# Attention's weighted values accumulated in PSUM bank 5 in place of bank 0

## The chip, the cores and the metric

The kernel runs on one core of a Trainium2 chip. The metric is device time in microseconds (us) of that core, the median of several executions. The engines named below are PE (TensorE, matmuls), ACT (ScalarE), DVE (VectorE), POOL (GpSimd) and SP (SyncE, which issues the DMAs). Each runs its own list of instructions in order and they meet through semaphores. PE writes its results into PSUM, of which this kernel uses eight banks of 128 x 512 floats.

## What is computed

A hybrid encoder trunk of two layers on 512 tokens of width 1024. In each layer one input projection feeds three mixers that run side by side: sliding-window attention with sinks, retention, and a Mamba-2 scan. Their outputs are concatenated and projected back; then comes a gated MLP. The part that the change touches is the attention:

```
def swa_sink_attention(q, k, v, sinks, attn_bias):
    ...
    logits = jnp.einsum('bcqhgd,bckhd->bchgqk', qc, kb).astype(jnp.float32) * (HEAD_DIM ** -0.5)
    logits = logits + attn_bias.reshape(A_KV_HEADS, G, CHUNK, A_WIN_CHUNKS * CHUNK)[None, None]
    ...
    p = jax.nn.softmax(jnp.concatenate([logits, sink], axis=-1), axis=-1)[..., :-1]
    out = jnp.einsum('bchgqk,bckhd->bcqhgd', p.astype(v.dtype), vb)
    return out.reshape(Bn, S, A_WIDTH)
```

The last einsum, the weighted values, is the step called AV. The retention reads its values centred over the head's width; that step is called RV.

## The kernel before

Activations lie with features on the 128 partitions and the 512 tokens along the free axis. A matrix product is done in "units" of one 128-wide block of output features: for each 128-wide block of the inner dimension three matmuls of 128 x 512, high part of the weights by high and by low part of the input, low part of the weights by high part of the input. The weights come by DMA in packs of four tiles into four slots (`w_raw`); ACT makes the high part `w_hi` (line 481), POOL the low part `w_lo` (line 378). Units write the two banks `dense0` and `dense1` in turn. All the mixers' small products share six further banks, `M[0]` to `M[5]` ("mix" in the profile).

The order on every engine comes from one hand-written list, `SCHEDULE` (line 80). Each engine walks through it once per layer and does its own share of each step, so that a step that is early in the list is early on every engine. D*n* are units of the projections. The piece in question, for each layer:

```
    "SB2 SA3 D16 D17 SB3 AS0 RV0 D18 RV1 AX0 D19 RV2 AT0 AS1 D20 RV3 AX1 AV0 D21 AT1 AS2 D22 AX2 AV1 "
    "SN0 D23 SX0 AT2 AS3 D24 AX3 AV2 SN1 D25 SX1 D26 AT3 RP0 D27 AV3 RP1 D28 RP2 D29 RP3 D30 RA0 D31 "
```

The attention works on four blocks of 128 queries, n = 0 to 3:

- AS*n*: PE computes scores into banks 0 and 1 and the transposed values into bank 4; DVE reads the scores out (line 910), takes the maximum and subtracts it (lines 920 to 926); ACT copies the values (line 580) and takes the exponentials (lines 583, 584).
- AX*n*: DVE sums, inverts and scales (lines 931 to 934).
- AT*n*: PE transposes the weights into banks 2 and 3; ACT copies them to `pt` (line 588).
- AV*n*: PE multiplies values and weights, four matmuls of 64 x 256 (line 1283), half of them on bank 2's copy and half on bank 3's; ACT splits off the high part (line 593, helper on line 498), DVE the low part (line 943), whose end frees the bank.

RV*n* is a step of the retention: PE multiplies one unit's result by a centring matrix into bank 5 (line 1296), ACT copies it to `vtok` (line 596), whose end frees the bank. RP*n* (rotary, bank 4; DVE line 954), RA*n* and RB*n* (retention; RA uses bank 0, RB bank 5 among others) follow. D20 to D23 are the scan's gate: DVE evacuates each (line 796), ACT takes its Silu (line 525), DVE multiplies it in (line 804), ACT squares the product (line 529). SN*n* sums squares in bank 4.

`BANKS` (line 96) says which banks a step uses. `bank_uses` numbers the uses of each bank in the order of `SCHEDULE`, and `take` (line 1095) lets PE wait until the use before has been read: `m_free[b]` counts the releases of bank b, `m_ready[b]` the results in it. ACT and DVE wait for the same numbers, through `ready`.

Of the kernel before, what the change touches and what calls it, by code (L numbers as in the profile page):

```python
# [88 lines left out]
def step_of(name):  # L89
# [5 lines left out]

BANKS = {
# [3 lines left out]
}  # L100

# [69 lines left out]
def build(nc, a, out):  # L171
    f32, f32r = mybir.dt.float32, mybir.dt.float32r
    ALU, ACT, AX = mybir.AluOpType, mybir.ActivationFunctionType, mybir.AxisListType
    with ExitStack() as ctx:
# [235 lines left out]
        def _(act):  # L410
# [60 lines left out]
            with act.Fori(0, DEPTH) as l:  # L471
# [28 lines left out]
                for name in SCHEDULE:  # L500
# [37 lines left out]
                    elif step == "TK":  # L538

                        act.wait_ge(dt_in, l + 1)  # L540
                        link(nc.scalar.activation(dt_e[:, :], dt_v[:, :], ACT.Abs))
                        nc.scalar.activation(exp_a[:, :], par["alog"][:, bass.ds(l * 8, 8)], ACT.Exp)
                        nc.scalar.activation(dt_e[:, :], dt_e[:, :], ACT.Exp, scale=-1.0).then_inc(dt_exp, 1)
                    elif step == "DTB":
                        act.wait_ge(dt_one, l + 1)
                        nc.scalar.activation(dt_u[:, :], dt_u[:, :], ACT.Ln).then_inc(dt_ln, 1)
                    elif step == "CM":
                        act.wait_ge(m_ready[5], ready(name, 1, l))
                        nc.scalar.activation(crows[:, 0, :], M[5][:, 0:P], ACT.Copy).then_inc(rows_done, 1)
                        nc.scalar.activation(crows[:, 1, :], M[5][:, 0:P], ACT.Exp).then_inc(m_free[5], 1)  # L550
                    elif step == "TOL":
                        act.wait_ge(wdec_in, l + 1)
                        nc.scalar.activation(wdec[:, :], wdec[:, :], ACT.Exp).then_inc(wdec_exp, 1)
                        lb = lastb[:, :].rearrange("p (b h) -> p b h", h=8)
                        for g in range(2):
                            rows = slice(64 * g, 64 * g + 64)
                            nc.scalar.activation(cdec[rows, :, :], lb[rows, :, 4 * g:4 * g + 4], ACT.Exp)\
                                .then_inc(cdec_done, 1)
                    elif step == "BC":
                        act.wait_ge(m_ready[0], ready(name, 0, l))  # L560
                        nc.scalar.activation(btok, M[0][:, :], ACT.Copy).then_inc(m_free[0], 1)
                    elif step == "SA":
                        for g in range(2):
                            act.wait_ge(l_in, l * 8 + 2 * n + g + 1)
                            lm = lms[:, n % 2, g]
                            nc.scalar.activation(lm, lm, ACT.Exp).then_inc(l_exp, 1)

                    elif step == "SN":
                        act.wait_ge(m_ready[4], ready(name, 0, l))
                        nc.scalar.activation(rs[:, :], M[4][:, :], ACT.Ln, scale=1.0 / 256,  # L570
                                             bias=par["eps"][:, 0:1]).then_inc(m_free[4], 1)
                        act.wait_ge(m_free[4], ready(name, 0, l) + 1)
                        nc.scalar.activation(rs[:, :], rs[:, :], ACT.Exp, scale=-0.5).then_inc(grs, 1)
                    elif step == "SX":
                        for t in (2 * n, 2 * n + 1):
                            act.wait_ge(gn_done, l * 4 + t + 1)
                            split_from(m_hi[:, t, :], xs[:, t, :], s_hi)
                    elif step == "AS":
                        act.wait_ge(m_ready[4], ready(name, 2, l))
                        nc.scalar.activation(vwin[:, n % 2, :, :], M[4][:, 0:2 * P].rearrange(  # L580
                            "p (c d) -> p c d", c=2), ACT.Copy).then_inc(m_free[4], 1)
                        act.wait_ge(lg_in, l * 4 + n + 1)
                        link(nc.scalar.activation(sk[:, :], sk[:, :], ACT.Exp))
                        nc.scalar.activation(lg, lg, ACT.Exp).then_inc(lg_exp, 1)
                    elif step == "AT":
                        for c in range(2):
                            act.wait_ge(m_ready[2 + c], ready(name, c, l))
                            nc.scalar.activation(pt[:, c, :], M[2 + c][:, :], ACT.Copy).then_inc(m_free[2 + c], 1)
                    elif step == "AV":
                        act.wait_ge(m_ready[0], ready(name, 0, l))  # L590
                        for c in range(2):
                            src = M[0][:, 256 * c:256 * c + 256].rearrange("p (t q) -> p t q", t=4)
                            split_from(m_hi[:, 4:8, CH * (2 * n + c):CH * (2 * n + c) + CH], src, a_hi)
                    elif step == "RV":
                        act.wait_ge(m_ready[5], ready(name, 0, l))
                        nc.scalar.activation(vtok[:, :, n, :], bank(5, 4), ACT.Copy).then_inc(m_free[5], 1)
                    elif step == "RB":
                        for j in range(2):
                            act.wait_ge(m_ready[3 + j], ready(name, j, l))
                            dst = ar("ry", 2, 2)[:, :, j, BLK * n:BLK * n + BLK]  # L600
                            nc.scalar.activation(dst, M[3 + j][:, 0:2 * P].rearrange("p (t s) -> p t s", t=2),
                                                 ACT.Copy).then_inc(m_free[3 + j], 1)
                    elif step == "RN":

                        if n == 0:
                            act.wait_ge(m_free[4], ready("RB3", 1, l) + 1)
                            for j in range(2):
                                nc.scalar.activation(sq[:, j, :], ry[:, j, :], ACT.Square).then_inc(r_sq, 1)
                        for j in range(2):
                            act.wait_ge(m_ready[j], ready(name, j, l))  # L610
                            nc.scalar.activation(rs2[j][:, :], M[j][:, :], ACT.Ln, scale=1.0 / P,
                                                 bias=par["eps"][:, 0:1]).then_inc(m_free[j], 1)
                        for j in range(2):
                            act.wait_ge(m_free[j], ready(name, j, l) + 1)
                            nc.scalar.activation(rs2[j][:, :], rs2[j][:, :], ACT.Exp, scale=-0.5)\
                                .then_inc(r_rs, 1)
                        if n == 0:
                            for j in range(2):
                                nc.scalar.activation(sq[:, j, :], ry[:, 2 + j, :], ACT.Square).then_inc(r_sq, 1)
                    elif step == "RX":  # L620
                        act.wait_ge(rn_done, l * 4 + n + 1)
                        split_from(m_hi[:, 8 + n, :], ry[:, n, :], r_hi)
# [39 lines left out]
        def _(dve):  # L662
# [58 lines left out]
            with dve.Fori(0, DEPTH) as l:  # L721
# [30 lines left out]
                for name in SCHEDULE:  # L752
# [183 lines left out]
                    elif step == "AV":  # L936
                        for c in range(2):
                            dve.wait_ge(a_hi, l * 8 + 2 * n + c + 1)
                            at = CH * (2 * n + c)
                            src = M[0][:, 256 * c:256 * c + 256].rearrange("p (t q) -> p t q", t=4)  # L940
                            if c == 0:
                                dve.wait_ge(a_hi, l * 8 + 2 * n + 2)
                            V.tensor_tensor(m_lo[:, 4:8, at:at + CH], src,
                                            m_hi[:, 4:8, at:at + CH].bitcast(f32), ALU.subtract)\
                                .then_inc(m_free[0] if c else a_lo, 1)
                    elif step == "RP":
                        r = (rk if n < 2 else rq)[:, n % 2, :]

# [95 lines left out]
        def _(pe):  # L1044
# [54 lines left out]
            with pe.Fori(0, DEPTH) as l:  # L1099
# [46 lines left out]
                for name in SCHEDULE:  # L1146
# [6 lines left out]
                    elif step == "D":  # L1153
                        if n < N_IN:
                            dense_unit(n, h_src)
                        else:
                            part = (n - N_IN) // 8
                            if n == N_IN:
                                pe.wait_ge(s_lo, l * 4 + 4)
                            elif n == N_IN + 8:  # L1160
                                pe.wait_ge(m_free[0], ready("AV3", 0, l) + 1)
                            dense_unit(n, m_src(4 * part), ret_tile if n == N_IN + 16 else None)
                    elif step == "NORM":
                        norm(l * 2, name, l)
# [111 lines left out]
                    elif step == "AV":  # L1276
                        take(name, 0, l)
                        for c in range(2):

                            pe.wait_ge(m_free[2 + c], ready(f"AT{n}", c, l) + 1)  # L1280
                            for g in range(2):
                                r = slice(64 * g, 64 * g + 64)
                                ins = mm(M[0][r, 256 * c:256 * c + 256], vwin[:, n % 2, c, r],
                                         pt[:, c, 256 * g:256 * g + 256])
                        ins.then_inc(m_ready[0], 1)
                    elif step == "RP":
                        r = (rk if n < 2 else rq)[:, n % 2, :]
                        pe.wait_ge(evac, l * N_EV + U_RK + n + 1)
# [243 lines left out]
```

## Time and profile before

| | us |
|---|---|
| median of three executions | 1305.99 |
| lowest, highest | 1304.16, 1306.04 |
| the profiled execution | 1307.44 |
| its span, first to last instruction | 1305.6 |
| PE busy | 1277.4 (98%) |
| DVE, ACT, POOL busy | 615.3, 565.3, 588.8 |

Matmuls are pipelined, so PE's busy time is not the time at its peak; where PE is idle the profile says what ended the idle time. The two layers show the same pattern some 639 us apart: the piece of `SCHEDULE` above is at about 130 to 217 us in the first, and at about 769 to 856 us in the second.

### The profile page before, as it was taken

What the parts mean: (1) busy time and instruction counts of PE and PEld (TensorE: products, weight loads), DVE (VectorE), ACT (ScalarE), POOL (GpSimd) and SP (SyncE); (2) the same over time, 40 slices, a digit from 0 to 9 for tenths busy, and PEclk for the clock granted to TensorE, in tenths of its full rate; (3) what the DMA queues carried; (4) which work ended last, traced back from release to release, by engine and by line L of the source; (5) the groups of instructions that cost most, each with busy time, mean ns of one, the idle gap of its engine ahead of it and who ended that gap; (6) DMA issues with size and microseconds to landing.
All of it is one profiled execution on the core that took longest, in us unless ns stands there. A gap on an engine that the chain in (4) does not pass through costs nothing.

```text
span 1305.6 us, 21212 instructions
## 1 busy us (share of the span) xinstructions
PE 1277.4 (98%) x6114; PEld 1032.3 (79%) x6114; DVE 615.3 (47%) x938; ACT 565.3 (43%) x902; POOL 588.8 (45%) x435
## 2 busy tenths in 40 slices
PE   7999999999999999999999999999999999999996
PEld 4888877778888888888878887777888888888885
DVE  6755666474444103332256556755653430133323
ACT  6432483465444223443344327726644332244433
POOL 4533434254444544554444443424455454455541
PEclk9999999999999999999999999999999999999998
DMA  7335212143333333333323432212333333333333
GB/s 221 91 111 137 74 56 74 49 112 90 96 96 96 97 97 97 96 96 90 98 89 89 131 106 73 76 47 67 91 111 98 96 101 97 91 96 97 96 95 113
DMA packets 77483, 125.29 MB, mean 96 GB/s; under 512 B 7752, under 2 KB 20456, under 8 KB 77288
## 3 DMA queue, kind: packets, MB, share of 16 engines
q1 hardware_dynamic: 77416, 124.43, 33.6%
q8 instruction: 38, 0.62, 0.2%
q14 instruction: 29, 0.24, 0.1%
HBM read 121.84 MB, written 2.55 MB: 95 GB/s over the span
## 4 chain that ended last, share of the span: by engine, by line
PE 83%; DVE 8%; ACT 4%; issue 4%; DMA 0%; DVEq 0%; SPq 0%; ACTq 0%
PE dense L1048 76%; PE mix L1048 6%; DVE h_lo L690 1%; ACT w_hi L481 1%; DVE arena L991 1%; DVE ssq L698 1%; DVE arena L739 1%; ACT L525 1%; DVE arena L993 1%; ACT m_hi L498 0%; DMA x<-in_xT 0%; DVE arena L910 0%; ACT pad L525 0%; DVE mx L920 0%; DVE arena L926 0%
## 5 line engine op out<-in xcount | busy, mean ns | idle before, releaser
L378 POOL TENSOR_TENSOR w_lo<-w_raw,w_hi 128x512 fp32r<-128x512 f32 x424 | 580.3, 1384 | 686.8 <-ACT w_hi L481 680.1
L1048 PE MATMUL dense<-h_hi,w_hi 128*128 128x512 f32 x1120 | 445.3, 398 | 3.9 <-DVE h_lo L690 3.0
L1048 PE MATMUL dense<-h_lo,w_hi 128*128 128x512 f32 x1120 | 437.3, 390 | 0.0
L481 ACT ACTIVATE w_hi<-w_raw 128x512 fp32r<-128x512 f32 x422 | 256.3, 627 | 258.4 <-PE dense L1048 242.4
L1048 PE MATMUL dense<-h_hi,w_lo 128*128 128x512 f32 x1120 | 300.5, 389 | 0.0
L1048 PEld LDWEIGHTS dense<-h_hi,w_hi 128*128 128x128 f32 x1120 | 211.0, 188 | 55.3 <-issue 10.0
L1048 PEld LDWEIGHTS dense<-h_lo,w_hi 128*128 128x128 f32 x1120 | 211.0, 188 | 45.2 <-issue 2.7
L1048 PEld LDWEIGHTS dense<-h_hi,w_lo 128*128 128x128 f32 x1120 | 210.4, 188 | 44.4
L1048 PE MATMUL dense<-m_hi,w_hi 128*128 128x512 f32 x544 | 217.3, 400 | 3.2 <-ACT w_hi L481 2.5
L1048 PE MATMUL dense<-m_lo,w_hi 128*128 128x512 f32 x544 | 212.0, 390 | 0.0
L1048 PE MATMUL dense<-m_hi,w_lo 128*128 128x512 f32 x544 | 146.9, 389 | 0.0
L1048 PEld LDWEIGHTS dense<-m_hi,w_hi 128*128 128x128 f32 x544 | 102.1, 188 | 28.9 <-DVE x L787 3.3
L1048 PEld LDWEIGHTS dense<-m_lo,w_hi 128*128 128x128 f32 x544 | 102.1, 188 | 23.0 <-issue 2.4
L1048 PEld LDWEIGHTS dense<-m_hi,w_lo 128*128 128x128 f32 x544 | 102.1, 188 | 21.4
L1029 DVE TENSOR_TENSOR x<-dense,x 128x512 f32<-128x512 f32 x32 | 22.1, 692 | 192.5 <-PE dense L1048 192.5
L1007 DVE TENSOR_TENSOR arena<-dense,rstd 128x512 f32<-128x512 f32 x44 | 30.5, 692 | 93.6 <-PE dense L1048 93.6
L641 ACT ACTIVATE arena<-arena 128x512 f32<-128x512 f32 x44 | 27.9, 634 | 85.9 <-DVE arena L1014 85.9
L1017 DVE TENSOR_TENSOR arena<-dense,rstd 128x512 f32<-128x512 f32 x44 | 30.4, 691 | 71.2 <-PE dense L1048 71.2
L1010 DVE SCALAR_TENSOR_TENSOR arena<-arena,params 128x512 f32<-128x512 f32 x44 | 35.7, 811 | 59.7 <-ACT arena L636 59.7
L1048 PE MATMUL mix<-arena 64*128 64x128 f32 (+4 forms) x696 | 56.6, 297 | 3.7 <-DVE arena L910 3.7
L423 ACT ACTIVATE h_hi<-x,params 128x512 fp32r<-128x512 f32 x39 | 28.3, 725 | 71.1 <-DVE x L1029 59.5
L1048 PEld LDWEIGHTS mix<-arena 128*64 128x64 f32 (+3 forms) x696 | 42.9, 160 | 17.1 <-issue 12.8
(173 smaller groups left out, 958.3 us busy)
## 6 DMA issues: line engine op xcount, KB each, us to landing
w_raw<-in_w SPq DMA_DIRECT2D x428, 256.0 KB, 2.6
arena<-cum_rows SPq DMA_DIRECT2D x8, 512.0 KB, 5.7
x<-in_xT SPq DMA_DIRECT2D x8, 256.0 KB, 6.3
out_y<-arena SPq DMA_DIRECT2D x8, 256.0 KB, 2.1
arena<-exp_rows SPq DMA_DIRECT2D x12, 128.0 KB, 6.4
consts<-in_consts SPq DMA_DIRECT2D x1, 1223.0 KB, 9.2
rel_scratch<-arena SPq DMA_DIRECT2D x1, 382.0 KB
bias<-rel_scratch SPq DMA_DIRECT2D x8, 32.0 KB, 2.5
```

What stands on the lines that cost most here:

```text
L378: nc.gpsimd.tensor_tensor(w_lo[:, s, :], w_raw[:, s, :], w_hi[:, s, :].bitcast(f32), ALU.subtract).then_inc(lo_ready, 1)
L423: nc.scalar.activation(h_hi[:, o, :], x[:, o, :], ACT.Copy, scale=gcol(e, o)).then_inc(h_hi_ready, 1)
L481: nc.scalar.activation(w_hi[:, slot, :], w_raw[:, slot, :], ACT.Copy).then_inc(hi_ready, 1)
L525: nc.scalar.activation(zt, zt, ACT.Silu).then_inc(z_silu, 1)
L641: nc.scalar.activation(fs, fy, ACT.Silu).then_inc(f_silu, 1)
L690: V.scalar_tensor_tensor(h_lo[:, o, :], x[:, o, :], gcol(e, o), h_hi[:, o, :].bitcast(f32), ALU.mult, ALU.subtract).then_inc(h_lo_ready, 1)
L698: V.tensor_tensor(ssq[:, :], ssq[:, :], sq[:, o % 2, :], ALU.add).then_inc(ssq_added, 1)
L1007: V.tensor_tensor(fpad[:, 2:2 + S], dense[0][:, :], rstd[:, :], ALU.mult).then_inc(evac, 1)
L1010: ins = V.scalar_tensor_tensor(fy, fpad[:, 1:1 + S], par["fconv"][:, bass.ds(fi * 4 + 1, 1)], fy, ALU.mult, ALU.add)
L1017: V.tensor_tensor(fb, dense[1][:, :], rstd[:, :], ALU.mult).then_inc(evac, 1)
L1029: V.tensor_tensor(x[:, o, :], dense[n % 2][:, :], x[:, o, :], ALU.add).then_inc(evac, 1)
L1048: return T.matmul(dst, lhsT, rhs, start=start, stop=stop)
```

## The change

AV is given bank 5 in place of bank 0: in the table, in PE's matmuls, in both readers and in the semaphores. No step moves in `SCHEDULE`.

```diff
@@ BANKS @@
-    "AS": (0, 1, 4), "AT": (2, 3), "AV": (0,), "RP": (4,), "RV": (5,), "SN": (4,),
+    "AS": (0, 1, 4), "AT": (2, 3), "AV": (5,), "RP": (4,), "RV": (5,), "SN": (4,),
@@ scalar, AV @@
-                        act.wait_ge(m_ready[0], ready(name, 0, l))
+                        act.wait_ge(m_ready[5], ready(name, 0, l))
...
-                            src = M[0][:, 256 * c:256 * c + 256].rearrange("p (t q) -> p t q", t=4)
+                            src = M[5][:, 256 * c:256 * c + 256].rearrange("p (t q) -> p t q", t=4)
@@ vector, AV @@
-                            src = M[0][:, 256 * c:256 * c + 256].rearrange("p (t q) -> p t q", t=4)
+                            src = M[5][:, 256 * c:256 * c + 256].rearrange("p (t q) -> p t q", t=4)
...
-                                .then_inc(m_free[0] if c else a_lo, 1)
+                                .then_inc(m_free[5] if c else a_lo, 1)
@@ tensor, D36 @@
-                                pe.wait_ge(m_free[0], ready("AV3", 0, l) + 1)
+                                pe.wait_ge(m_free[5], ready("AV3", 0, l) + 1)
@@ tensor, AV @@
-                                ins = mm(M[0][r, 256 * c:256 * c + 256], vwin[:, n % 2, c, r],
+                                ins = mm(M[5][r, 256 * c:256 * c + 256], vwin[:, n % 2, c, r],
                                          pt[:, c, 256 * g:256 * g + 256])
-                        ins.then_inc(m_ready[0], 1)
+                        ins.then_inc(m_ready[5], 1)
```

PE's order at RV3 and AV0, before. `mix5` and `mix0` are banks 5 and 0; `dense1` is D21.

```order
L1048 MATMUL mix5<-consts,pad 128x128 [waits mix5_free]
L1048 MATMUL mix5<-consts,pad 128x128 x3
L1097 REGISTER_ALU
L1280 REGISTER_ALU [waits mix0_free]
L1048 MATMUL mix0<-arena 64x256 [waits mix2_free]
L1048 MATMUL mix0<-arena 64x256
L1048 MATMUL mix0<-arena 64x256 [waits mix3_free]
L1048 MATMUL mix0<-arena 64x256
L1048 MATMUL dense1<-h_hi,w_hi 128x512 [waits w_hi_ready,unit_evacuated]
```

The same place now:

```order
L1048 MATMUL mix5<-consts,pad 128x128 [waits mix5_free]
L1048 MATMUL mix5<-consts,pad 128x128 x3
L1097 REGISTER_ALU
L1280 REGISTER_ALU [waits mix5_free]
L1048 MATMUL mix5<-arena 64x256 [waits mix2_free]
L1048 MATMUL mix5<-arena 64x256
L1048 MATMUL mix5<-arena 64x256 [waits mix3_free]
L1048 MATMUL mix5<-arena 64x256
L1048 MATMUL dense1<-h_hi,w_hi 128x512 [waits w_hi_ready,unit_evacuated]
```

No instruction moved on PE; the wait ahead of AV0's first matmul is for bank 5, which RV3's matmuls wrote last, where it was for bank 0.

ACT's order at the same place, before: the Silu of D20, the square, the copy of RV3, and the two splits of AV0.

```order
L525 ACTIVATE pad<-pad 128x512 [waits unit_evacuated]
L529 ACTIVATE sq<-arena 128x512 [waits yg_done]
L595 REGISTER_ALU
L596 ACTIVATE arena<-mix5 128x4x128 [waits mix5_ready]
L590 REGISTER_ALU
L498 ACTIVATE m_hi<-mix0 128x4x64 [waits mix0_ready]
L498 ACTIVATE m_hi<-mix0 128x4x64
```

And now:

```order
L529 ACTIVATE sq<-arena 128x512 [waits yg_done]
L595 REGISTER_ALU
L596 ACTIVATE arena<-mix5 128x4x128 [waits mix5_ready]
L590 REGISTER_ALU
L498 ACTIVATE m_hi<-mix5 128x4x64 [waits mix5_ready]
L498 ACTIVATE m_hi<-mix5 128x4x64
```

Here too nothing moved; the splits read bank 5 and wait for it. On DVE the only difference beside the bank's name is that three register instructions are gone, since the numbers that two waits compare with have become equal.

## Rows read from the trace of the kernel before

**Rows 1.** The page's part 4, shares of the chain that ended last.

```profile
PE 83%; DVE 8%; ACT 4%; issue 4%; DMA 0%; DVEq 0%; SPq 0%; ACTq 0%
```

**Rows 2.** PE's waits: line, releaser: us in total, times, longest.

```profile
PE mix L1048 <- DVE arena L910: 3.7, 2, 1.8
PE mix L1048 <- DVE ssq L698: 3.4, 1, 3.4
```

**Rows 3.** PE's timeline, layer one: start, length, operation [idle before].

```profile
151.93 1.05 PE L1048 MATMUL mix<-consts,pad 128*128 128x128 f32 x8
152.91 1.08 PE L1048 MATMUL mix<-arena 128*64 128x256 f32 x8
...
159.58 1.09 PE L1274 MATMUL mix<-consts,arena 128*128 128x128 f32 x8
...
184.81 1.08 PE L1048 MATMUL mix<-arena 128*64 128x256 f32 x8 [1.84 <-DVE arena L910]
```

**Rows 4.** ACT's timeline, layer one.

```profile
156.73 0.64 ACT L529 ACTIVATE sq<-arena 128x512 f32<-128x512 f32 x1 [0.93 <-DVE arena L804]
157.27 0.58 ACT L596 ACTIVATE arena<-mix 128x512 f32<-128x512 f32 x1
...
160.82 0.63 ACT L525 ACTIVATE pad<-pad 128x512 f32<-128x512 f32 x1 [0.47 <-DVE pad L796]
...
182.35 1.07 ACT L588 ACTIVATE arena<-mix 128x512 f32<-128x512 f32 x2
...
202.97 1.07 ACT L588 ACTIVATE arena<-mix 128x512 f32<-128x512 f32 x2
```

**Rows 5.** DVE's timeline, layer one.

```profile
152.21 0.69 DVE L796 TENSOR_TENSOR pad<-dense,rstd 128x512 f32<-128x512 f32 x1 [1.78 <-PE dense L1048]
...
160.10 0.68 DVE L796 TENSOR_TENSOR pad<-dense,rstd 128x512 f32<-128x512 f32 x1
...
207.88 0.68 DVE L954 TENSOR_TENSOR ssq<-mix,consts 128x512 f32<-128x512 f32 x1
```

**Rows 6.** The chain in order of time, 182 to 186: start, us, what.

```profile
184.08 0.61 DVE arena L910
184.69 0.12 issue
```

**Rows 7.** PE's timeline, layer two.

```profile
792.21 1.08 PE L1048 MATMUL mix<-arena 128*64 128x256 f32 x8
...
824.11 1.08 PE L1048 MATMUL mix<-arena 128*64 128x256 f32 x8 [1.84 <-DVE arena L910]
```

**Rows 8.** ACT's timeline, layer two.

```profile
796.57 0.58 ACT L596 ACTIVATE arena<-mix 128x512 f32<-128x512 f32 x1
```

**Rows 9.** PE's timeline further on in layer one.

```profile
205.01 1.08 PE L1048 MATMUL mix<-arena 128*64 128x256 f32 x8
...
209.76 1.02 PE L1048 MATMUL mix<-arena,consts 128*128 128x512 f32 x2
```

**Rows 10.** PE's timeline near the start of the program.

```profile
24.02 1.77 PE L1048 MATMUL mix<-ssq,consts 128*128 128x512 f32 x2 [3.36 <-DVE ssq L698]
```

**Rows 11.** Stretches: PE, PEld, DVE, ACT, POOL busy; granted clock, DMA share, GB/s.

```profile
22.00:24.00 2.00, 0.00 (x0) 0.00 (x0) 1.97 (x5) 1.92 (x2) 2.00 (x2) 1.00 0.65 115
24.00:25.00 1.00, 0.98 (x3) 0.57 (x3) 1.00 (x2) 0.00 (x0) 1.00 (x2) 0.68 0.43 48
25.00:26.00 1.00, 1.00 (x2) 0.40 (x2) 0.09 (x1) 0.17 (x1) 1.00 (x2) 0.50 0.44 49
26.00:27.00 1.00, 1.00 (x4) 0.80 (x3) 0.00 (x0) 0.98 (x2) 0.24 (x1) 0.50 0.52 78
27.00:28.00 1.00, 1.00 (x5) 0.76 (x4) 0.00 (x0) 0.99 (x2) 0.00 (x0) 0.61 0.70 147
...
180.00:183.00 3.00, 2.97 (x14) 2.12 (x12) 2.96 (x4) 2.46 (x5) 1.74 (x1) 1.00 0.59 156
185.00:188.00 3.00, 3.00 (x16) 1.79 (x14) 2.90 (x6) 0.00 (x0) 0.00 (x0) 1.00 0.00 0
```

## The prediction

> **What bounds the kernel now.** I read the chain of work that ended last, then TensorE's list of waits, then the timelines of the three engines round the changed steps. The chain lies on PE for 83% of the span, and so do nearly all of its costs [rows 1]. What matters here is where PE is not the bound. Its list of waits is short: the one on VectorE's line 910 is 3.7 us in two pieces, one for each of the two layers [rows 2]. The timeline puts the first piece in front of the matmuls at 184.81, which are AV2, with 1.84 us idle [rows 3]; the second is at 824.11, again 1.84 us [rows 7]. So AV2 waits for a release of bank 0: in bank 0 the scores of AS3 still lie when PE comes to AV2, and VectorE's line 910 reads them late. Otherwise PE runs through this part without a gap: RV3 at 151.93, AV0 at 152.91, the projection D21 up to the transposes AT1 at 159.58 [rows 3].
>
> A bank that is written again must first have been read. For AV0 in bank 5 the last reader before it is ScalarE's copy of RV3 (line 596), and the place of that copy in ScalarE's order is the point of this case.
>
> **What goes: the wait at AV2.** AV2 no longer needs bank 0. In bank 5 it needs AV1 read, which both engines have read before AT2 starts. What is late next is its own operand, the two copies of AT2 to SBUF by ScalarE, at 182.35 for 1.07 us together [rows 4]. PE was through with D24 at 184.81 - 1.84 = 182.97; the first copy ends about 182.89 and the second at 183.42. AV2's first half would start at 183.0 and the second at 183.5, so against the trace of before the whole 1.84 us go except a tenth or so. That is -1.84 a layer; how the copies stand after the other part of the change is worked out below.
>
> **What comes: a wait at AV0.** RV3 and AV0 stand next to one another on PE, RV3 at 151.93 and AV0 at 152.91 [rows 3]. ScalarE copies RV3's result only at 157.27, for 0.58 us, so it ends at 157.85 [rows 4]. It is so late because in ScalarE's own order there stand ahead of it the exponentials of AS1, four copies of weights, the Silu of D20 and the square at 156.73, and this square had to wait 0.93 us for VectorE [rows 4]. None of these depends on AV0, so the copy doesn't move. From a release to PE's start the trace has 0.12 us, behind the read at 184.08 [rows 6]. AV0 then starts at 157.85 + 0.12 = 157.97 in place of 152.91: **+5.06 us**. In the second layer the copy runs from 796.57 for 0.58 us [rows 8] and AV0 stood at 792.21 [rows 7]: 797.15 + 0.12 - 792.21 = 5.06 again. Nothing covers this wait: behind AV0 in PE's order stand D21, AT1 and all the rest, though D21 has its weights and needs nothing of AV0.
>
> **Does the new wait move the other engines too?** The chain that used to release AV2 begins at D21: evacuation by VectorE at 160.10 [rows 5], Silu by ScalarE at 160.82 [rows 4], then AS2, AX2, and so to the copies of AT2. The evacuation at 160.10 did not wait for PE; VectorE came to it 0.3 us later than PE allowed (AT1's start at 159.58 plus some 0.28, as D20's evacuation came 0.28 behind RV3's start: 152.21 against 151.93 [rows 3, 5]). With D21 5.06 later it follows PE at once, at 159.58 + 5.06 + 0.28 = 164.92, hence VectorE and ScalarE are late by 4.8 us and PE by 5.06. Where PE came to AV2 at 182.97 it now comes at 188.03, and the first copy of AT2 is there at 182.89 + 4.8 + 0.12 = 187.8, the second at 188.3, when PE's first half is just through. So AV2 waits for nothing: of the 1.84 us the whole goes, and PE is 5.06 - 1.84 = **3.22 us** late behind it, VectorE and ScalarE still 4.8.
>
> **What is late next.** With the other two 1.6 us further behind PE than before, two places have less slack than that. AV3 at 205.01 [rows 9] needs the first copy of AT3, which ended about 202.97 + 0.54 = 203.51 [rows 4]: now 203.51 + 4.8 + 0.12 = 208.4, PE comes at 208.2, a wait of 0.15 to 0.2. RP2 at 209.76 [rows 9] needs bank 4, read at 207.88 for 0.68 us [rows 5]: now free at 208.56 + 4.8 + 0.12 = 213.5, PE comes at 209.76 + 3.22 + 0.15 = 213.1, a wait of 0.3. Together I take **0.45 us**; between 0 (if those engines catch up a little) and 1 (if a weight split also comes late). Behind RP3 VectorE waits for PE again, so nothing more is handed on. From there to the end of the layer the work is PE's, and a delay goes through whole.
>
> AV0's other edges cost nothing: its matmuls now end at 157.97 + 1.08 = 159.05 [rows 3], so the two splits that ScalarE made right behind its copy come some 1.2 us later, in time in which ScalarE would only wait for D21. On VectorE three register instructions fall away, too short to be seen. RB0 now takes bank 5 behind AV3 in place of RV3; four projections lie between the two.
>
> **The clock.** The new gap is 157.97 - 152.98 = 5.0 us without a matmul. The trace has one gap like it inside the kernel: the matmul at 24.02 has 3.36 us idle ahead of it, so the one before ended at 20.66 [rows 10], and in the four microseconds from 24 the granted clock is 0.68, 0.50, 0.50 and 0.61: it sits at 1.2 in place of 2.4 GHz for 3.4 us, and 0.32 + 0.50 + 0.50 + 0.39 = 1.71 us of work at full clock are lost [rows 11]. From 22 to 24 it was still full [rows 11]. On both sides of the gap of 1.84 us at AV2 it is 1.00 [rows 11]. A gap of 5.0 is on the far side of 3.36, so I expect the fall, twice. Its price: not above 1.71 as far as the row shows; in that row the fall came about 3.7 us behind the last matmul, which would here lie 1.3 us inside the gap, where it costs nothing, leaving 2.1 us at half rate or 1.06. The bounds are 0 (it holds) and 1.71; I take the middle of 1.06 and 1.71, **1.4 us** a layer.
>
> The Trainium skill, "TensorE: Matmul & The Clock Gate", section "HAM oscillation — how this bites in real kernels", tells of a kernel with waits of 3 to 5 us between bursts, 53.3 us throttled over 32 gaps. That is 1.67 us a gap, of which half is lost, 0.83; with that estimate the sum below would end at 1314.9 in place of 1316.1. No row here shows a gap of 5 us.
>
> **The sum.** A layer: +5.06 - 1.84 + 0.45 + 1.4 = +5.07; two layers: +10.1. The profiled execution took 1307.44 (span 1305.6); it would be 1317.6. It stands 1.45 above the median of the runs, 1305.99, so the median becomes **1316.1 us**, 0.8% slower.
>
> **The rivals.**
> 1. The clock holds at one gap or at both. For it: when the clock falls against the gap is seen once only. Without either fall: 1305.99 + 2 x 3.67 = 1313.3; with one 1314.7.
> 2. The new lag of VectorE and ScalarE costs more than 0.45: D27's weights (the split copies by ScalarE come just as PE needs them) or AV3 lose a microsecond more a layer. 1318.1, and 1318.7 with the clock's full price.
> 3. On the other side, faster: the wait at AV2 goes and that at AV0 stays small. It decides at the end of the copy of RV3: the two parts cancel where the copy ends 5.06 - 1.84 = 3.2 us earlier, at 154.6. If it ended before 152.8, AV0 would wait for nothing and the time would be 1305.99 - 3.7 = 1302.3. Against it: ScalarE is busy without a gap from the exponentials to the Silu in the trace, and the copy stands behind them in a fixed order.
> 4. The change does nothing visible, because AV0's wait lies under one that PE has anyway: 1306. Against it: PE shows no idle time between 151.93 and 159.58.
>
> **How the numbers follow.** Both gaps cold, near 1316.1: 0.58. Rival 1: 0.24 (one gap 0.15, none 0.09). Rival 2: 0.13. Rival 3: 0.03. Rival 4: 0.02. The range reaches over the forecast, rival 1 with the 1 us by which runs of this kernel differ, and nearly all of rival 2: 1312.6 to 1318.6. About 0.2%, or 2.6 us, is what a measurement of this kernel can tell from no change; slower by more than that holds in the forecast and rivals 1 and 2: 0.95, the same 0.02, faster 0.03.
>
> **What would show it.** In the profile of the changed kernel: the list of waits has PE waiting for ScalarE's line 596 twice, 5 us each, in front of the matmuls that write 128x256 into a mix tile for the first time in a layer; the wait on line 910 is gone; the granted clock is near 0.5 for some microseconds behind each gap, in D21's matmuls. ScalarE's line 596 for RV3 stays at 157.3. AV2 shows no idle time, AV3 and RP2 some tenths. I am wrong if the copy of RV3 is found earlier than 157, if the idle time at AV2 persists beside the new one (then 3.7 us more), or if the clock stays at 1.00.

## The result, and the profile of the changed kernel

| | before | changed |
|---|---|---|
| median, us | 1305.86 (4 runs) | 1317.11 (4 runs) |
| lowest, highest | 1304.16, 1306.04 | 1316.52, 1318.99 |
| profiled execution, its span | 1307.44, 1305.6 | 1318.99, 1317.2 |

The ratio of the changed kernel to the one before is 1.0092, with a 95% interval of 1.0074 to 1.0109: 0.9% slower, 11 us. It is the direction that was forecast, and 1317.11 lies inside the range, 1.0 above the forecast of 1316.1. The profiled execution of the kernel before, 1307.44, is not one of its four.

PE's list of waits (line, releaser: us in total, times, longest) is what answers to [rows 2]:

```profile
PE mix L1048 <- ACT arena L596: 9.9, 2, 4.9
...
PE mix L1048 <- DVE ssq L698: 2.3, 1, 2.3
...
PE mix L1048 <- ACT arena L588: 0.6, 2, 0.3
```

The line on VectorE's 910 is gone, and at the top of the list stands the wait for the copy of RV3, once a layer. The timeline of PE in the first layer answers to [rows 3] and [rows 9]:

```profile
150.76 1.05 PE L1048 MATMUL mix<-consts,pad 128*128 128x128 f32 x8
156.74 1.97 PE L1048 MATMUL mix<-arena 128*64 128x256 f32 x8 [4.93 <-ACT arena L596]
...
166.20 1.03 PE L1274 MATMUL mix<-consts,arena 128*128 128x128 f32 x8
...
189.46 1.12 PE L1048 MATMUL mix<-arena 128*64 128x256 f32 x8
...
210.06 1.14 PE L1048 MATMUL mix<-arena 128*64 128x256 f32 x8 [0.30 <-ACT arena L588]
...
215.06 1.13 PE L1048 MATMUL mix<-arena,consts 128*128 128x512 f32 x2
```

From top to bottom: RV3; AV0 with its new idle time; AT1; AV2, now without idle time; AV3; RP2. Measured from one row to the next, against the same distance before:

| first layer | before, us | changed, us | difference |
|---|---|---|---|
| RV3 to AV0 | 0.98 | 5.98 | +5.00 |
| AV0 to AT1 | 6.67 | 9.46 | +2.79 |
| AT1 to AV2 | 25.23 | 23.26 | -1.97 |
| AV2 to AV3 | 20.20 | 20.60 | +0.40 |
| AV3 to RP2 | 4.75 | 5.00 | +0.25 |

That sums to +6.47. The second layer has the same pattern, RV3 at 796.44 and AV0 at 802.43:

```profile
796.44 1.05 PE L1048 MATMUL mix<-consts,pad 128*128 128x128 f32 x8
802.43 1.98 PE L1048 MATMUL mix<-arena 128*64 128x256 f32 x8 [4.93 <-ACT arena L596]
...
811.62 1.03 PE L1274 MATMUL mix<-consts,arena 128*128 128x128 f32 x8
```

Here AV0 to AT1 is 9.19 us, where before it was 798.88 - 792.21 = 6.67: +2.52. From RV3 of one layer to RV3 of the next it is 645.68 us; before, 639.29 (791.22, where RV3 of the second layer stood, less 151.93): +6.39. From there to the end of the span it is 520.76 against 514.38: +6.38. The part up to the first RV3 was 1.17 us shorter in this execution (150.76 against 151.93), so the spans differ by 11.6.

ScalarE's timeline answers to [rows 4]:

```profile
152.70 1.28 ACT L525 ACT_TABLE_LOAD   x1
153.99 0.63 ACT L525 ACTIVATE pad<-pad 128x512 f32<-128x512 f32 x1
155.50 0.63 ACT L529 ACTIVATE sq<-arena 128x512 f32<-128x512 f32 x1 [0.88 <-DVE arena L804]
156.04 0.58 ACT L596 ACTIVATE arena<-mix 128x512 f32<-128x512 f32 x1
158.76 0.66 ACT L498 ACTIVATE m_hi<-mix 128x256 fp32r<-128x256 f32 x2 [2.14 <-PE mix L1048]
```

The copy did not move: it starts 5.28 us behind RV3's start, where it started 5.34 behind it before. AV0 follows its end by 0.12. The first row belongs to what keeps the copy back, and the prediction's list of the work ahead of it leaves it out: in front of the Silu of D20 ScalarE loads a function table for 1.28 us. And the stretches round the gap (the number ahead of the last two is the granted clock) answer to [rows 11]:

```profile
152.00:156.00 4.00, 0.00 (x0) 0.00 (x0) 1.34 (x2) 3.10 (x5) 4.00 (x4) 1.00 0.46 122
156.00:157.00 1.00, 0.26 (x2) 0.26 (x4) 0.93 (x3) 0.62 (x2) 0.59 (x1) 0.53 0.59 184
157.00:162.00 5.00, 5.00 (x16) 3.20 (x15) 2.01 (x4) 0.66 (x2) 0.00 (x0) 0.50 0.27 79
162.00:163.00 1.00, 1.00 (x5) 0.77 (x3) 0.00 (x0) 0.00 (x0) 0.00 (x0) 0.56 0.00 0
163.00:164.00 1.00, 1.00 (x6) 0.83 (x5) 0.00 (x0) 0.35 (x1) 0.00 (x0) 1.00 0.00 0
```

The clock falls about 156.06 (0.53 over that microsecond is 0.06 at full and 0.94 at half rate), before PE starts again, and is back about 162.88 (0.56 is 0.88 at half). It sits at 1.2 GHz in place of 2.4 for 6.8 us, twice the 3.4 us of the low stretch in [rows 11] that set the price in the prediction. In the second layer it does the same from 801.18 to 808.00, with PE starting again at 802.43.

### The profile page after: what moved, and what is told of

It is laid out like the page before. It is cut to its first block, busy times and chain, and to the rows that moved or that the text cites. A ratio compares the mean times of both kernels' runs of the same rounds, so it can differ in the third digit from the quotient of the medians.

```text
span 1317.2 us, 21210 instructions
## 1 busy us (share of the span) xinstructions
PE 1283.6 (97%) x6114; PEld 1036.1 (79%) x6114; DVE 623.5 (47%) x938; ACT 564.4 (43%) x902; POOL 586.3 (45%) x435
## 4 chain that ended last, share of the span: by engine, by line
PE 82%; DVE 8%; ACT 5%; issue 4%; DVEq 0%; DMA 0%; ACTq 0%; SPq 0%
PE dense L1048 75%; PE mix L1048 6%; DVE h_lo L690 1%; ACT w_hi L481 1%; ACT m_hi L498 1%; DVE arena L991 1%; DVE ssq L698 1%; DVE arena L739 1%; ACT L525 1%; DVE arena L993 1%; ACT L534 0%; ACT L570 0%; DVE mx L920 0%; DVE arena L926 0%; DVE arena L1039 0%
```

## The experiments

Eight runs were made beside the kernel before. Runs one to four take the sum apart, runs five, six and eight ask about the clock, and run seven is the changed kernel once more. Where a run gives a distance from RV3, it is that of the first layer of its profiled execution.

### One: the gap filled with work

```diff
@@ tensor, AV, ahead of take @@
+                        if n == 0:
+                            pe.wait_ge(m_free[0], ready("AS1", 0, l) + 1)
+                            for k in range(20):
+                                mm(M[0][:, :], h_hi[:, 0, 0:P], h_hi[:, k % KD, :])
                         take(name, 0, l)
```

> The changed kernel with 20 matmuls of 128x512 without use, written to bank 0 (free at that time) between RV3 and AV0 of each layer, about 4.6 us of work inside the 4.93 us in which PE waits for the copy of RV3. AV0 starts when it did. Theory A, the time lost between AV0 and AT1 (AV0 to AT1 took 9.46 and 9.19 us, before 6.67) is the fallen clock: the granted clock stays at 1.00, AV0 to AT1 takes about 6.7 us again, and the time falls by 2.8 + 2.5 = 5.3 us from 1317.1 to about 1311.8, still 6 above the kernel before. Theory B, bank 5 or the late readers make D21 itself slow (weights not ready, a bank shared by two readers): AV0 to AT1 stays at 9.2 to 9.5 and the time at 1317.

Measured: 1312.21 (1312.05 to 1312.48), ratio to before 1.0048 (1.0032 to 1.0063). PE's timeline:

```profile
148.79 1.05 PE L1048 MATMUL mix<-consts,pad 128*128 128x128 f32 x8
149.60 4.79 PE L1048 MATMUL mix<-h_hi 128*128 128x512 f32 x20
154.84 1.08 PE L1048 MATMUL mix<-arena 128*64 128x256 f32 x8 [0.45 <-ACT arena L596]
...
161.46 1.03 PE L1274 MATMUL mix<-consts,arena 128*128 128x128 f32 x8
```

and the stretches round the filled gap in each layer:

```profile
150.00:165.00 15.00, 14.55 (x84) 11.41 (x83) 6.91 (x11) 7.08 (x13) 7.34 (x7) 1.00 0.35 91
797.00:812.00 15.00, 14.55 (x83) 11.43 (x82) 8.94 (x14) 7.21 (x14) 4.82 (x4) 1.00 0.29 79
```

AV0 starts 6.05 us behind RV3, as late as in the changed kernel, but AV0 to AT1 takes 6.62 us (6.59 in the second layer), at a granted clock of 1.00. So the 2.79 and 2.52 us that the changed kernel lost between AV0 and AT1 were the clock: theory A. The kernel does 40 matmuls more than the changed one and is 4.9 us faster by the medians. From RV3 of the first layer to RV3 of the second it is 643.26 us, 3.97 above before, which the table above gives without its second row: 5.00 - 1.97 + 0.40 + 0.25 = 3.7. By the medians the two layers together are only 6.05 above before (1312.21 against 1306.16), where the distances give 7.9. The part up to the first RV3 differs from execution to execution: RV3 stands at 148.79 here and at 151.93 in [rows 3], and between 147.83 and 151.93 over the ten profiled executions.

### Two: the copy of RV3 earlier

```diff
@@ scalar, D @@
                         hi_to(SEGS[n][-1][0] + 2)
+                        if n == 20:
+                            act.wait_ge(m_ready[5], ready("RV3", 0, l))
+                            nc.scalar.activation(vtok[:, :, 3, :], bank(5, 4), ACT.Copy).then_inc(m_free[5], 1)
                         if awaited:
@@ scalar, RV @@
-                    elif step == "RV":
+                    elif step == "RV" and n < 3:
```

> The changed kernel, in which ScalarE copies RV3 two weight packs after the exponentials of AS1, ahead of the other two packs, the Silu of D20 and the square, in place of behind them. PE's matmuls and all banks are those of the changed kernel. Theory A, the place of this copy in ScalarE's order is the whole cause: the copy starts at about RV3's end + 0.1, PE waits some 0.8 us at AV0, the clock stays at 1.00, AV2's wait stays away, all of ScalarE's chain is 0.6 to 0.9 later; a layer comes to about +0.9 - 1.7 + 0.4, the time to 1305 (1304 to 1306.5), level with the kernel before or a little below. Theory B, AV in bank 5 costs through something else too (RV, AV and RB in one bank, the splits of AV behind PE): above 1308.

Measured: 1305.11 (1304.0 to 1308.88, 11 runs), ratio 0.9998 (0.9989 to 1.0007). AV is in bank 5 throughout, and the 11 us are gone. PE:

```profile
148.84 1.05 PE L1051 MATMUL mix<-consts,pad 128*128 128x128 f32 x8
150.66 1.08 PE L1051 MATMUL mix<-arena 128*64 128x256 f32 x8 [0.76 <-ACT arena L518]
157.72 1.09 PE L1277 MATMUL mix<-consts,arena 128*128 128x128 f32 x8 [0.32 <-DVE arena L937]
...
181.10 1.14 PE L1051 MATMUL mix<-arena 128*64 128x256 f32 x8
...
201.72 1.14 PE L1051 MATMUL mix<-arena 128*64 128x256 f32 x8 [0.31 <-ACT arena L591]
```

The wait at AV0 is 0.76 us, as worked out, and AV2 has none. Against before AV0 is 0.84 late, AT1 1.23, AV2 0.62 early, AV3 0.20 early. What was not in the expectation is the wait of 0.32 at AT1: the Silu of D20 now stands behind the copy and starts 4.04 us behind RV3 in place of 3.23, VectorE starts the last operation of AX1 7.60 behind it in place of 6.37, and AT1 needs its result. Theory A holds, with that term on top; theory B, that bank 5 costs by itself, falls. This is the condition of the forecast's rival 3 made real. With the copy early the time is that of before within the interval, and the sign depends on tenths.

### Three and four: the two halves of the change

The bank is given for each AV by a table, `AV_BANK`, that the matmuls, the readers and the semaphores use in place of the entry in `BANKS`. Run three has

```diff
+AV_BANK = (0, 5, 5, 5)
...
+def banks_of(name):
+    head, n = step_of(name)
+    return (AV_BANK[n],) if head == "AV" else BANKS.get(head, ())
```

> AV0 in bank 0 as in the kernel before, AV1 to AV3 in bank 5. Theory A: no wait for the copy of RV3, the clock stays, the wait of 1.84 us at AV2 goes in each layer but VectorE and ScalarE are then that much further behind PE, and AV3 and RP2 wait 0.3 and 0.25 us and may lose a little more: -1.84 + 0.6 a layer, the time at 1303.5 (1302.3 if these two waits don't come). Theory B, the 1.84 us were only VectorE's and ScalarE's lateness and come back whole at the next step that needs them: 1305.9, as before.

and run four

```diff
+AV_BANK = (5, 0, 0, 0)
```

> AV0 in bank 5 as in the changed kernel, AV1 to AV3 in bank 0 as in the kernel before. Theory A: wait of 4.93 us at AV0 and the fallen clock as in the changed kernel, and AV2 waits for VectorE's read of AS3 again. VectorE and ScalarE follow D21 0.25 us closer than they did, so AV2's wait is 1.6 us and AV2 starts 7.3 to 7.6 us later than before in each layer; AV3 and RP2 wait for nothing. 1305.9 + 7.5 + 7.3 = 1320.7. Theory B, the wait at AV2 was covered by the one at AV0 whatever the bank: 1317.

Measured: three, 1303.20 (1301.58 to 1305.87, 11 runs), ratio 0.9982 (0.9973 to 0.9991). Four, 1320.77 (1319.13 to 1323.04, 4 runs), ratio 1.0114 (1.0097 to 1.0132). PE's waits of run three and, in the second fence, of run four:

```profile
PE mix L1056 <- DVE ssq L706: 2.3, 1, 2.3
...
PE mix L1056 <- ACT arena L596: 0.6, 2, 0.3
```

```profile
PE mix L1056 <- ACT arena L604: 9.9, 2, 4.9
PE mix L1056 <- DVE arena L918: 3.5, 2, 1.7
```

The line numbers are shifted by the table: in both, L596 is the copy of AT, L604 that of RV3, L918 VectorE's read of AS. Run three has neither large wait, only the 0.3 at AV3: AV2 stands 1.87 us earlier behind RV3 than before, AV3 1.45 earlier, RP2 1.19 earlier. So of the 1.84 us two thirds stay a gain, and one third is given back further on, where VectorE and ScalarE are the later ones. Run four has both waits, 4.93 at AV0 and 1.73 at AV2, and AV2 is 7.61 us later behind RV3 than before. So the wait at AV2 is not covered by the one at AV0: VectorE and ScalarE are moved with PE, because their chain starts at D21. Theory B falls in both runs. The sum of the halves is the whole: -2.96 (three) and +14.6 (four), by medians, together +11.6, against +11.2 for the change. By distances in the first layer it is the same: behind RV3, RP2 stands 1.19 earlier in run three and 7.60 later in run four, together +6.41, where the changed kernel has +6.47.

Run four's profiled execution has something more in its second layer. There too AV2 waits 1.73 us, and 1.4 us behind its restart the clock falls, at 837.26, for 3.4 us:

```profile
835.84 1.08 PE L1056 MATMUL mix<-arena 128*64 128x256 f32 x8 [1.73 <-DVE arena L918]
```

```profile
837.00:838.00 1.00, 1.00 (x3) 0.49 (x3) 0.93 (x4) 0.00 (x0) 0.00 (x0) 0.63 0.00 0
838.00:840.00 2.00, 2.00 (x5) 1.33 (x4) 1.70 (x2) 0.83 (x2) 0.00 (x0) 0.50 0.00 0
840.00:841.00 1.00, 1.00 (x4) 0.78 (x3) 0.54 (x1) 1.00 (x3) 0.00 (x0) 0.66 0.00 0
```

From AV2 to AT3 it takes 14.54 us there, against 12.88 in the first layer, where the same wait had no fall behind it. AV2 itself is 6.76 later behind RV3 in that layer, less than the 7.3 expected. So that 1320.77 meets the expected 1320.7 so closely is in part luck.

Run three is also the version that is better than both kernels. It takes the half of the change that pays and is 0.18% faster than the kernel before, with an interval that leaves out 1.

### Five to eight: the clock

All four are on the changed kernel and share seven new runs of the kernel before (1305.16). Run seven is the changed kernel itself:

> The changed kernel itself on this chip, for comparison: 1317 (1316 to 1319), gaps of 4.93 us and low stretches of the clock of 3.4 or 6.8 us.

Measured: 1316.61 (1314.85 to 1319.63), ratio 1.0088 (1.0069 to 1.0107). Its profiled execution has the gap at AV0 (4.92 and 4.93 us), the low stretch of 6.8 us and AV0 to AT1 at 9.54 and 9.21 us in the two layers.

Runs five and six have the filling of run one with `range(9)` and with `range(5)`:

> The changed kernel with 9 useless matmuls of 128x512 in bank 0 right behind RV3, about 2.1 us of work, so that some 2.8 us of the 4.93 us gap at AV0 stay idle. AV0 starts when it did, D21 too if the clock holds. Theory C, the clock falls in proportion to nothing but a long enough idle stretch, and 2.8 us (less than the 3.36 us in front of the norm of the first layer) is too short in most executions: 1312.2 as with the full filling, granted clock 1.00. Theory D, 2.8 us is enough: some 1317, or between the two if only one layer or part of the executions falls.

> The same with 5 useless matmuls, 1.1 us of work, 3.8 us idle. Theory C: 3.8 us is more than the 3.36 us after which the clock fell in front of the first norm, so it falls here in both layers, in a low stretch of 3.4 us as there (1.7 us lost a layer, 1315.6) or of 6.8 us as in the changed kernel (2.6, 1317.5). Theory D, the fall depends on where the gap lies in time rather than on its length: executions spread between 1312 and 1317.

Measured: five, 1315.99 (1314.26 to 1316.93), ratio 1.0085 (1.0068 to 1.0102); six, 1317.39 (1315.73 to 1317.54), ratio 1.0089 (1.0072 to 1.0106). Idle in front of AV0 were 2.91 and 3.80 us. The stretches of run five in the first layer, where AV0 starts at 153.85:

```profile
150.00:155.00 5.00, 2.09 (x14) 1.07 (x13) 3.17 (x5) 2.82 (x5) 3.71 (x3) 1.00 0.60 160
155.00:156.00 1.00, 1.00 (x3) 0.83 (x4) 0.67 (x2) 0.64 (x2) 0.00 (x0) 0.58 0.64 231
156.00:158.00 2.00, 2.00 (x6) 1.55 (x5) 0.49 (x2) 0.00 (x0) 0.00 (x0) 0.50 0.02 8
158.00:159.00 1.00, 1.00 (x4) 0.79 (x4) 0.00 (x0) 0.00 (x0) 0.00 (x0) 0.71 0.00 0
```

and of run six, where AV0 starts at 155.19:

```profile
152.00:154.00 2.00, 0.00 (x0) 0.00 (x0) 0.92 (x2) 1.09 (x3) 2.00 (x3) 1.00 0.62 180
154.00:155.00 1.00, 0.00 (x0) 0.00 (x0) 1.00 (x1) 1.00 (x2) 1.00 (x1) 0.77 0.71 205
155.00:161.00 6.00, 5.81 (x17) 3.92 (x18) 2.39 (x6) 0.72 (x3) 0.04 (x1) 0.50 0.32 83
161.00:162.00 1.00, 1.00 (x5) 0.78 (x5) 0.00 (x0) 0.00 (x0) 0.00 (x0) 0.82 0.00 0
```

In run five the clock falls at about 155.16, after PE has started again, stays low for 3.4 us, and AV0 to AT1 takes 8.18 us in place of 6.67: 1.5 lost. In run six it falls at 154.54, still in the gap, stays low for 6.8 us, and AV0 to AT1 takes 9.47: 2.8 lost. The second layer has the same lengths in both runs (falls at 800.28 and 799.66, 3.4 and 6.8 us low). Run five's theory C, that 2.8 us idle is short enough, falls: 2.91 us were enough for a fall in both layers, at a lower price than in the changed kernel. In run six the longer of theory C's two low stretches is the one that came, with its time of 1317.5. Run six's theory D, executions spread between 1312 and 1317, isn't seen in its four. Run five's median lies 3.8 us above run one's, where its profile shows 2 x 1.5; the profiled execution, 1314.26, is the fastest of its four, and what the others add is not known.

Run eight leaves the gap whole and puts the work behind it:

```diff
@@ tensor, AV @@
+                        if n == 0:
+                            pe.wait_ge(m_free[0], ready("AS1", 0, l) + 1)
                         take(name, 0, l)
+                        if n == 0:
+                            for k in range(12):
+                                mm(M[0][:, :], h_hi[:, 0, 0:P], h_hi[:, k % KD, :])
```

> The changed kernel with 12 useless matmuls of 128x512 behind the wait for bank 5 and ahead of AV0, so nothing fills the gap of 4.93 us, and PE restarts with full-size matmuls in place of AV0's small ones. Theory E, the small matmuls of AV0 keep the clock low: with the full-size ones the low stretch is 3.4 us. Theory F, what is small or large plays no part and the low stretch stays at 6.8 us. In both the 12 matmuls add work: 12 x 0.43 us where the clock is low all through them, 5.1 us a layer, in place of AV0 and D21 falling into the low stretch; with F the loss by the clock is as before and the time 1317.1 + 2 x 12 x 0.23 = 1322.6; with E it is 1.5 us less a layer, 1319.6.

Measured: 1322.80 (1321.1 to 1323.12), ratio 1.0131 (1.0114 to 1.0147). The clock in the first layer, PE starting again at 154.75:

```profile
151.00:154.00 3.00, 0.00 (x0) 0.00 (x0) 1.26 (x2) 2.11 (x3) 3.00 (x3) 1.00 0.54 152
154.00:155.00 1.00, 0.25 (x1) 0.25 (x2) 0.93 (x3) 0.70 (x2) 0.68 (x1) 0.52 0.77 143
155.00:160.00 5.00, 5.00 (x12) 3.55 (x12) 1.34 (x2) 0.00 (x0) 0.00 (x0) 0.50 0.26 90
160.00:161.00 1.00, 1.00 (x7) 0.56 (x8) 0.00 (x0) 0.00 (x0) 0.00 (x0) 0.57 0.00 0
```

Low from 154.04 to 160.86: 6.8 us with full-size matmuls too, and again from 802.56 to 809.40. Theory E falls: that AV0's own matmuls are small plays no part in how long the clock stays low here. The time is that of theory F, 1322.6.

## Why the prediction was right, and which of its terms was not

- **The place of the wait and its cause** held as told: 4.93 us twice in front of AV0, released by ScalarE's line 596, AV0 5.00 us later behind RV3 where 5.06 was worked out. Run two moved nothing but that copy, and the wait became 0.76. The list of what stands ahead of the copy lacked the table load of 1.28 us, which changes no number, since the copy's place was read from its own row.
- **The wait at AV2 goes** held: AT1 to AV2 is 1.97 shorter for the 1.84 forecast, and run three, with that half alone, shows AV2 1.87 earlier.
- **VectorE and ScalarE move with PE** held. Run four shows it from the other side: with AV2 back in bank 0 the wait is 1.73, where it was 1.84.
- **What is late next** held in its places and was a little small: 0.40 + 0.25 = 0.65 a layer for 0.45. AV3's wait for the copies of AT3 is 0.30 in the list for the 0.15 to 0.2 of the working. RP2's share shows as a distance only; the list has no wait there.
- **That the clock falls, twice,** held, and run one shows that nothing else lies between AV0 and AT1. **Its price was mis-sized**: 1.4 a layer, with 1.71 as the upper bound, against 2.79 and 2.52 measured. The step that failed is the one from [rows 11] to the bound. There the low stretch was 3.4 us and the prediction took that length as given, and even let a part of it lie inside the gap for nothing. In the changed kernel the clock fell inside the gap and stayed low for 6.8 us; in the first layer 6.1 of these lay behind PE's restart. Half of that would be 3.07 us, and 2.79 were lost. The "full price" of one row was not a ceiling.
- **The sum**: 5.07 a layer was forecast and 6.39 measured, the 1.3 between them being almost wholly the clock (2.65 for 1.4). By that the medians would have differed by 12.8, and the changed kernel would have taken 1318.6, at the edge of the range; they differ by 11.2. The profiled executions show a difference of that size in their first 150 us, where RV3 stood 1.17 earlier. That the median of 1317.11 came within 1.0 of the forecast is partly luck.
- The estimate by the Trainium skill, "TensorE: Matmul & The Clock Gate", section "HAM oscillation — how this bites in real kernels", was 0.83 us a gap. This case's trace differs: 2.52 and 2.79 for gaps of 4.93, 1.5 for one of 2.91. The measurement decides. That PE comes out of such waits at the low clock, which the page tells of its kernel, agrees: it did so behind both gaps of 4.93. (By the prediction's own terms the sum with 0.83 ends at 1315.0; it says 1314.9.)
- **Of the rivals**, 1 (the clock holds) is not seen in either of the two profiled executions of the changed kernel. 2 is right in a small part, 0.65 a layer for 0.45. 3 needs the earlier copy of run two. Its lower end, a copy that ends before 152.8 and a time of 1302.3, was out of reach by the prediction's own rows: the copy can't start before RV3's matmuls end at 152.98, and run two, with the copy about as early as it can be, still waited 0.76. 4 falls.

## What to carry to other kernels

When a step is given another buffer, look for the last reader of that buffer in front of it, and find where that read stands in its own engine's order: the matmuls of RV3 and AV0 were neighbours on PE, but the read between them stood behind 5 us of other work and waiting on ScalarE. A rebinding of several steps should be judged step by step, since here one of four carried the whole loss and another the whole gain. And a wait of some microseconds on PE has to be priced with the clock behind it, and one low stretch in a trace does not bound that price: here the trace of before showed 3.4 us low, and 6.8 came.

## What the runs showed of the chip that was not expected

- The low stretches came in two lengths, 3.4 and 6.8 us (the end of the program left out), and where the clock fell went with the length in all cases but one. It fell behind PE's restart and stayed low 3.4 us in [rows 10, 11] (idle 3.36 us), at the start of the changed kernel's execution (idle 2.27), in both layers of run five (idle 2.91) and in the second layer of run four (idle 1.73). It fell 0.50 to 2.45 us ahead of the restart and stayed low 6.8 us in both layers of the changed kernel, of its repeat and of runs four, six and eight (idle 3.80 to 4.93), however much work came behind. The exception is the start of run three. There it fell about 22.64, 0.28 ahead of the restart, and stayed low 3.4 us:

```profile
22.92 2.07 PE L1056 MATMUL mix<-ssq,consts 128*128 128x512 f32 x2 [2.30 <-DVE ssq L706]
```

```profile
22.00:23.00 1.00, 0.08 (x1) 0.08 (x1) 1.00 (x4) 0.84 (x1) 1.00 (x2) 0.82 0.73 168
23.00:26.00 3.00, 3.00 (x5) 1.75 (x6) 1.00 (x1) 0.95 (x2) 2.14 (x2) 0.50 0.51 55
26.00:27.00 1.00, 1.00 (x5) 0.75 (x4) 0.00 (x0) 1.00 (x1) 0.00 (x0) 0.97 0.70 159
```

So a fall ahead of the restart does not by itself mean the long stretch. What sets the two lengths was not tested and stays open.

- Idle stretches of one length had different ends. In front of the first norm, 2.27 us (the changed kernel) and 2.30 us (run three) had a fall, and 2.32 (run two), 2.54 (run one), 2.76 (run seven), 2.91 (run eight) and 2.94 (run four) had none, while 2.91 at AV0 had one in both layers of run five. Run four's two waits of 1.73 ended one way in the first layer and the other in the second. Length alone doesn't decide between 1.7 and 3 us. What a fall in front of the first norm costs shows in the distance from that norm's matmuls to those of line 1048 that read `x`: 28.30 - 22.86 = 5.44 us in the changed kernel, 26.38 - 22.58 = 3.80 in run eight.
- That such falls are a part of why executions of one kernel differ by 2 to 4 us is argued and fits the clocks on record. Of the 21 executions of the kernel before beside runs one to four, the nine with a mean granted clock of 0.997 took 1304.58 to 1305.62 us, and the twelve with 0.996 or 0.995 took 1306.05 to 1308.43. Run one, whose gaps at AV0 are filled, spread over 0.4 us in its four executions, though four are few.
